# Two transformer blocks on one core: latent attention's values unit before the exponentials, a rotary unit in another bank, a gate exponential moved

## What is computed

```python
def _mla(x, w_in, g_q, g_kv, w_uq, w_uk, w_uv, w_o, pos):
    h = x @ w_in
    c_q = _rmsnorm(h[..., :384], g_q)
    c_kv = _rmsnorm(h[..., 384:640], g_kv)
    k_r = _rope(h[..., 640:], pos)
    q = jnp.einsum('bsr,rhd->bshd', c_q, w_uq)       # 8 heads, 128 + 64
    q_n, q_r = q[..., :128], _rope(q[..., 128:], pos)
    # keys c_kv @ w_uk, values c_kv @ w_uv, 128 per head;
    # causal softmax of (q_n.k_n + q_r.k_r) * 192**-0.5, times the values, @ w_o
```

## Time and profile before

| what | us |
|---|---|
| median of 3 runs | 2496.05 (2494.08 to 2497.16) |
| the profiled execution | 2496.92 |
| its span in the profile | 2495.1 |
| PE busy | 2433.2 (98%) |
| DVE busy | 1120.0 (45%) |
| ACT busy | 885.0 (35%) |
| mean granted clock of PE | 0.989 |

### The profile page before, as it was taken

One profiled execution on the slowest core, in us unless ns is written; L12 is line 12 of the kernel. 1 busy time (PEld: TensorE's weight loads), 2 busy tenths in 40 slices (PEclk: granted clock), 3 DMA queues, 4 the chain that ended last, 5 costly groups with the idle time before them and its releaser, 6 DMA issues.

```text
span 2495.1 us, 29378 instructions
## 1 busy us (share of the span) xinstructions
PE 2433.2 (98%) x11724; PEld 2015.2 (81%) x11724; DVE 1120.0 (45%) x1536; ACT 885.0 (35%) x1449; POOL 72.4 (3%) x146
## 2 busy tenths in 40 slices
PE   8889999999989999998999999999999999999998
PEld 7668888888878888887888888888877888888887
DVE  4556543346656443347454322233246624433334
ACT  4333332233534232235344323332245534522222
POOL 3000000000000000000000000000000000000000
PEclk9989999999989999999999999999999999999999
DMA  4121523323202322332222232222321122332332
GB/s 137 37 85 51 190 97 101 101 86 111 75 17 85 118 91 95 101 102 68 68 84 69 100 101 85 84 68 86 105 68 52 52 100 77 110 101 85 101 101 68
DMA packets 177048, 219.05 MB, mean 88 GB/s; under 512 B 9987, under 2 KB 131040, under 8 KB 176816
## 3 DMA queue, kind: packets, MB, share of 16 engines
q1 hardware_dynamic: 173152, 204.82, 25.4%
q0 software_dynamic: 3792, 12.75, 1.6%
HBM read 215.43 MB, written 5.27 MB: 88 GB/s over the span
## 4 chain that ended last, share of the span: by engine, by line
PE 92%; DVE 5%; ACT 2%; issue 1%; DMA 0%; SPq 0%; DVEq 0%; ACTq 0%
PE A L533 46%; PE B L533 42%; DVE WL L1871 1%; PE C L533 1%; ACT WH L1287 1%; PE C L955 0%; DVE ar L1939 0%; PE C L813 0%; DVE Y L2059 0%; PE C L1177 0%; DMA X<-in_x 0%; PE C L1015 0%; PE A L658 0%; DVE XL L1886 0%; DVE X L2477 0%
## 5 line engine op out<-in xcount | busy, mean ns | idle before, releaser
L1871 DVE TENSOR_TENSOR WL<-RAW,WH 128x2048 fp32r<-128x2048 f32 (+3 forms) x197 | 439.2, 2229 | 646.7 <-ACT WH L1287 646.5
L1287 ACT ACTIVATE WH<-RAW 128x2048 fp32r<-128x2048 f32 (+3 forms) x197 | 366.9, 1863 | 610.7 <-PE A L533 555.9
L533 PE MATMUL B<-XH,WH 128*128 128x512 f32 (+1 forms) x1432 | 544.4, 384 | 4.9 <-ACT ar L1290 2.6
L533 PE MATMUL B<-XH,WL 128*128 128x512 f32 (+1 forms) x1432 | 536.2, 378 | 0.0
L533 PE MATMUL B<-XL,WH 128*128 128x512 f32 (+1 forms) x1432 | 521.3, 379 | 2.8 <-DVE XL L1886 2.5
L533 PE MATMUL A<-WH,YH 128*128 128x512 f32 x944 | 368.0, 390 | 1.6 <-DVE YL L2404 1.6
L533 PE MATMUL A<-WH,YL 128*128 128x512 f32 x944 | 367.6, 389 | 0.0
L533 PE MATMUL A<-WL,YH 128*128 128x512 f32 x944 | 367.5, 389 | 0.0
L533 PEld LDWEIGHTS B<-XH,WH 128*128 128x128 f32 x1432 | 270.0, 189 | 72.5 <-issue 17.1
L533 PEld LDWEIGHTS B<-XH,WL 128*128 128x128 f32 x1432 | 270.1, 189 | 50.6
L533 PEld LDWEIGHTS B<-XL,WH 128*128 128x128 f32 x1432 | 260.7, 189 | 52.9 <-DVE XL L1886 4.8
(11 more groups left out here) (304 smaller groups left out, 2122.5 us busy)
## 6 DMA issues: line engine op xcount, KB each, us to landing
RAW<-in_w_in SPq DMA_DIRECT2D x33, 1024.0 KB, 5.2
RAW<-in_mlp_w_up SPq DMA_DIRECT2D x32, 1024.0 KB, 5.3
RAW<-in_mlp_w_down SPq DMA_DIRECT2D x32, 1024.0 KB, 5.0
RAW<-in_w_in SPq DMA_DIRECT2D x48, 512.0 KB, 4.4
RAW<-in_w_ffn_in SPq DMA_DIRECT2D x22, 1024.0 KB, 5.1
RAW<-in_w_ffn_out SPq DMA_DIRECT2D x10, 1024.0 KB, 5.0
RAW<-in_mla_w_o SPq DMA_DIRECT2D x4, 1024.0 KB, 5.1
RAW<-in_swa_w_q SPq DMA_DIRECT2D x4, 1024.0 KB, 5.1
```

The source lines that it names most:

```text
L533: return nc.tensor.matmul(dst, l, r, start=first, stop=last)
L1287: nc.scalar.activation(WH[s][:, 0:n], RAW[s][:, 0:n], ACT.Copy).then_inc(hi_ready, 1)
L1871: tt(WL[s][:, 0:n], RAW[s][:, 0:n], f32(WH[s][:, 0:n]), ALU.subtract).then_inc(lo_ready, 1)
```

## The change

1. `queries_by_feature` takes a list. Blocks 0 and 1 are transposed where all three were; block 2 comes inside `in_keys(1)`, behind its first token block.
2. Unit 4 of pair 0 has no number any more and lies in bank A3; its semaphore is `rope_taken`. The other units move up by one, so pair 0's units 2 and 5 lie in B0 and 3 and 6 in B1, and ten units alternate in place of eleven (`PAIR_AHEAD`).
3. Before the loop ACT splits the first chunk of pair 1 ahead of taking out unit 5, and DVE ahead of taking out unit 6; DVE normalises block 0 before the maxima of block 1.
4. In the loop ACT takes out a unit (0, 2 or 5) before the exponentials of step j+2, and in steps 1, 5 and 9 DVE makes the maxima before it splits.
5. At the start of the mLSTM ACT copies the two feature banks and splits a chunk before it makes the gates' exponential.

```diff
     def unit_number(i, u):
-        return PAIR_UNITS * i + tuple(units_in_order(i)).index(u)
+        return PAIR_UNITS * i - 1 + u if i else (0, 1, 2, 3, None, 4, 5)[u]
...
     def unit_bank(n):
-        return n % 2 if n < PAIR_AHEAD else 0
+        if n is None:
+            return A[3]
+        return B[n % 2 if n < PAIR_AHEAD else 0]
...
-    PAIRS, PAIR_STEPS, PAIR_UNITS, PAIR_AHEAD, PART_STEPS = 4, 16, 7, 11, (10, 11, 13, 14)
+    PAIRS, PAIR_STEPS, PAIR_UNITS, PAIR_AHEAD, PART_STEPS = 4, 16, 7, 10, (10, 11, 13, 14)
...
                 elif kh == 1:
                     r.then_inc(s_("in_kv"), 1)
+                    if t == 0:
+                        queries_by_feature((2,))
...
-        queries_by_feature()
+        queries_by_feature((0, 1))
         in_keys(1)
...
-            if n >= PAIR_AHEAD:
-                pe.wait_ge(*unit_taken(n - 1))
+            if n is None:
+                pass
+            elif n >= PAIR_AHEAD:
+                pe.wait_ge(*unit_taken(n - (2 if n == PAIR_AHEAD else 1)))
...
         # ACT
         pair_unit(0, 2)
+        split(c0 + 2, more=16 * 2 + 128)
         pair_unit(0, 5)
-        split(c0 + 2, more=16 * 2 + 128)
         pair_exp(0)
...
-            if j + 2 < PAIR_STEPS:
-                pair_exp(j + 2)
             for u in us[:1]:
                 if u in (0, 2, 5):
                     pair_unit(i, u)
+            if j + 2 < PAIR_STEPS:
+                pair_exp(j + 2)
             pair_hi(j)
...
+        before_conv(0, 0)
+        split_pair("ml", 0, 0, False)
         act.wait_ge(s_("if_m"), 1)
         nc.scalar.activation(G_EM, G_EM, ACT.Exp, scale=-1.0).then_inc(s_("if_g"), 1)
-        before_conv(0, 0)
-        split_pair("ml", 0, 0, False)
         after_conv(0, 0)
...
         # DVE
-        for u in (4, 3, 6):
-            pair_unit(0, u)
+        pair_unit(0, 4)
+        pair_unit(0, 3)
         split(c0 + 2)
+        pair_unit(0, 6)
         pair_max(0)
         pair_unit(1, 1)
         split(c0 + 3)
+        pair_normal(0)
         pair_max(1)
         pair_unit(1, 3)
-        pair_normal(0)
...
             pair_weights(j)
+            if j + 2 < PAIR_STEPS:
+                pair_max(j + 2)
             if j in (1, 5, 9):
                 split(c0 + 4 + j // 2)
-            if j + 2 < PAIR_STEPS:
-                pair_max(j + 2)
```

More of the change, by code:

```diff
@@ L239, in slot, with place_in_pair @@
         return c % 2
-    def units_in_order(i):
-        return (0, 1, 4, 2, 3, 5, 6) if i == 0 else range(PAIR_UNITS)
     def unit_number(i, u):
-        return PAIR_UNITS * i + tuple(units_in_order(i)).index(u)
+        return PAIR_UNITS * i - 1 + u if i else (0, 1, 2, 3, None, 4, 5)[u]
+    def place_in_pair(i, u):
+        return u if i else (0, 1, 3, 4, 2, 5, 6)[u]
     def wait_unit(e, i, u):
-        at = unit_number(i, u) - PAIR_UNITS * i
+        at = place_in_pair(i, u)
         if at in (4, 6):
@@ L257, in unit_bank @@
     def unit_bank(n):
-        return n % 2 if n < PAIR_AHEAD else 0
+        if n is None:
+            return A[3]
+        return B[n % 2 if n < PAIR_AHEAD else 0]
     def unit_taken(n):
+        if n is None:
+            return s_("rope_taken"), 2
         if n < PAIR_AHEAD:
             return s_("pair_u%d" % (n % 2)), n // 2 + 1
-        return s_("pair_u0"), (PAIR_AHEAD + 1) // 2 + n - PAIR_AHEAD + 1
+        return s_("pair_u0"), PAIR_AHEAD // 2 + n - PAIR_AHEAD + 1
     def units_of(j):
@@ L714, in in_keys, with queries_by_feature @@
                     r.then_inc(s_("in_kv"), 1)
-        def queries_by_feature():
-            for k in range(3):
+                    if t == 0:
+                        queries_by_feature((2,))
+        def queries_by_feature(ks):
+            for k in ks:
                 u = n0 + 2 + k
@@ L756, in pair_unit @@
             sl, n = slot(c), unit_number(i, u)
-            bank = B[unit_bank(n)]
+            bank = unit_bank(n)
             if u in (0, 5):
                 pe.wait_ge(lo_ready, c + 1)
-            if n >= PAIR_AHEAD:
-                pe.wait_ge(*unit_taken(n - 1))
+            if n is None:
+                pass
+            elif n >= PAIR_AHEAD:
+                pe.wait_ge(*unit_taken(n - (2 if n == PAIR_AHEAD else 1)))
             elif n >= 2:
@@ L770, in pair_unit @@
                     for k in range(2):
-                        if n == 5 and x == 0:
+                        if n == 4 and x == 0:
                             pe.wait_ge(c_free[(in_c + 5 + k) % 2], (in_c + 5 + k) // 2 + 1)
@@ L780, in pair_unit @@
                 for k in range(nk):
-                    if n < 5:
+                    if i == 0:
                         cu = in_c + 2 + x0 + k
@@ L784, in pair_unit @@
                     r = mm3(bank[:], wh[:, k, at:at + P], wl[:, k, at:at + P], YH[:, x0 + k, :], YL[:, x0 + k, :], k == 0, k == nk - 1)
-            r.then_inc(chunk_done if n - PAIR_UNITS * i in (4, 6) else s_("pair_f"), 1)
+            r.then_inc(chunk_done if place_in_pair(i, u) in (4, 6) else s_("pair_f"), 1)
         def pair_scores(j):
@@ L791, in pair_scores @@
             if q == 0:
-                for x in (3, 4):
-                    pe.wait_ge(*unit_taken(PAIR_UNITS * i + x))
+                for u in (2, 3):
+                    pe.wait_ge(*unit_taken(unit_number(i, u)))
                 pe.wait_ge(s_("qr_ready"), i + 1)
@@ L819, in pair_values @@
                 for u in (5, 6):
-                    pe.wait_ge(*unit_taken(PAIR_UNITS * i + u))
+                    pe.wait_ge(*unit_taken(unit_number(i, u)))
             if j == 0:
-                pe.wait_ge(*unit_taken(PAIR_AHEAD - 2))
+                pe.wait_ge(*unit_taken(PAIR_AHEAD - 1))
             pe.wait_ge(s_("pair_lo"), j)
@@ L836, in output_part @@
                 pe.wait_ge(lo_ready, c + 1)
-                pe.wait_ge(*unit_taken(PAIRS * PAIR_UNITS - 1))
+                pe.wait_ge(*unit_taken(unit_number(PAIRS - 1, PAIR_UNITS - 1)))
                 pe.wait_ge(s_("pair_lo"), 8)
```

## The result

| | before | changed |
|---|---|---|
| median | 2495.12 us of 4 runs (2494.08 to 2497.16) | 2464.61 us of 4 runs (2463.94 to 2468.89) |
| the profiled execution | 2496.92 | 2468.89 |
| span | 2495.1 | 2467.1 |
| granted clock, mean | 0.989 | 0.993 |

The ratio is 0.988, with a 95% interval of 0.9868 to 0.9891: faster by 1.2%. The forecast was 2468.0 with a range of 2464.5 to 2474.0. Profile against profile, as the sum was made, the gain is 2496.92 - 2468.89 = 28.0 us against a sum of 28.4.

What follows compares the result with a forecast made beforehand. TensorE (PE) was taken as the bound, so only its waits and slow clock give time back. Gains 1.1 + 4.6 + 1.3 + 17.3 + 4.1 = 28.4 us off 2496.9 gave 2468.5, written as 2468.0 for the median; range 2464.5 to 2474.

Steps and rivals of the forecast that it cites:

- (a): Query latents: third transposition behind the first token block of in_keys(1) removes PE's wait for bank C0; gain 1.1 us.
- (b): First pair: rotary unit in A3 and earlier splits remove waits and clock loss, leaving a new 0.8 us wait; gain 4.6.
- (c): First normalisation on DVE ahead of the second maxima and unit 3's copy in pair 1 removes PE's wait; gain 1.3 us.
- (d): Loop steps 1, 5, 9: ACT copies unit 5 before exponentials, so long waits and slow clock go; gain 17.3 us together.
- (e): Start of the mLSTM: bank copies ahead of the gates' exponential remove PE's 2.6 us wait and 1.5 of clock; gain 4.1.
- a long wait is thus paid twice: Behind PE's long waits the clock is 0.51 to 0.65, a second payment of 1.5 to 2.6 us each.
- the 0.9 us between execution and median: Whole kernel: the profiled execution lies 0.9 us above the runs' median, so 2468.5 would be a median of 2467.6.
- 1, the clock low behind short waits: First pair and loop: clock stays low behind waits of 0.2 to 0.8 us, 8.5 us not returned, 2477; chance 0.07.
- 2, DVE in ACT's place: Loop: unit 6's copy ends a filled DVE queue, 1 us more delay in three steps, 2471 to 2472; chance 0.09.
- 3, part (e) without gain: Start of the mLSTM: copies wait for something else or ACT is late for the first head, 2472; chance 0.04.
- 4, exponentials behind the units: Loop steps 1, 2, 3, 5, 6, 7: PE comes to wait for delayed exponentials, slower at 2502; chance 0.01.

Runs made afterwards that it cites:

- the gates' run: Kernel before with only the gates' exponential moved behind the two bank copies and the split: 2490.11 us, ratio 0.9983.
- ACT's half: Kernel before with only ACT's loop order changed, the unit taken out before the exponentials of step j+2: 2479.64 us, ratio 0.9936.
- DVE's half: Kernel before with only DVE's loop order changed, maxima ahead of the split: 2485.38 us, ratio 0.996.
- both halves: Kernel before with the loop's ACT and DVE orders both changed and nothing else: 2475.69 us, ratio 0.992.
- the kernel with four copies: Changed kernel with four copies of a small constant onto itself on ACT before taking out unit 5 in steps 1, 5, 9: 2464.22 us, ratio 0.9882.

## Why the prediction was right

Part by part, from PE's timelines. A row is a distance between two places in PE's program, and its difference is the gain there:

| part | from, to | before | after | gain | forecast |
|---|---|---|---|---|---|
| (a) | transposed latents (C, L723) to unit 0 | 8.41 | 7.05 | 1.4 | 1.1 |
| (b) | unit 0 to unit 0 of pair 1 | 19.44 | 14.81 | 4.6 | 4.6 |
| (c) | from there to its rotary unit | 13.21 | 11.46 | 1.8 | 1.3 |
| (d) | values(j) to the next unit 0, step 1 | 10.09 | 4.79 | 5.3 | 5.2 |
| | the same, step 5 | 10.88 | 4.78 | 6.1 | 6.1 |
| | the same, step 9 | 11.18 | 5.15 | 6.0 | 6.0 |
| (e) | from the splits, in the gates' run | 52.8 | 48.4 | 4.4 | 4.1 |

These make 29.6 us; less the 1.8 at 1100 us they are 27.8, where the profiles differ by 28.0.

**Right: the order of what is late next.** Part (b) forecast a new wait of 0.8 us behind unit 5, from DVE's chain of two instructions of 0.7; it is 0.79 (0.79 and 0.78 in the two runs that change the first pair alone). Part (d) forecast leftovers of 0.2, 0.2 and 0.6; they are 0.17, 0.18 and 0.54. What made this possible is that each queue is filled around these places, so the durations of the earlier trace rows could simply be added up.

**Slightly off: (a) and (c)**, 0.3 and 0.5 us too small: the term was mis-sized since I counted only the wait that the profile names, and a wait costs more. PE's timeline around it in the kernel before:

```profile
79.06 0.39 PE L533 MATMUL B<-YH,WL 128*128 128x512 f32 x1
80.72 0.69 PE L813 MATMUL C<-ident,ar 128*128 128x128 f32 x2 [1.27 <-DVE ar L1984]
81.25 0.81 PE L533 MATMUL A<-ar 128*128 128x384 f32 x2
```

and in the changed kernel:

```profile
73.65 0.40 PE L537 MATMUL B<-YH,WL 128*128 128x512 f32 x1
73.88 0.38 PE L821 MATMUL C<-ident,ar 128*128 128x128 f32 x2
```

with the scores right behind at 74.10. From the last product to the transposes it was 1.66 us and is 0.23: 1.27 of wait and 0.16 by which matmuls that follow each other overlap. From the transposes to the scores it was 0.53 and is 0.22: the first instructions behind a wait run 0.31 longer. Together 1.27 + 0.16 + 0.31 = 1.74, the gain measured. In (a) it is 1.13 + 0.16 and 0.06 at the transposes (0.41 from 44.76 to the next block, now 0.35 from 45.50).

**Off in kind, though not in sum: "a long wait is thus paid twice".** I took the clock's part as a fixed price of each long wait, 10.0 us of the 28.4. For this pair of profiles that holds to a few tenths. But the runs show it is no fixed price: the first pair's wait of 2.2 us costs 1.7 us of clock in the kernel before, and nothing in those with ACT's half, DVE's half, both halves or the gates alone, where nothing ahead of it was changed. In the one with ACT's half 1.7 us were lost behind the split's wait of 1.6 us instead, which I had counted as free. So 1.7 us of part (b)'s 4.6 depend on the execution that they are compared with. A sum over parts tried alone is wrong by 2.7 us in 28 for that reason.

**The median.** 30.5 us of gain against 28.0 between the profiles: the other three executions of the changed kernel lie 4.0 to 5.0 us below the profiled one, at mean clocks of 0.995 to 0.996 against its 0.993. The second profile of the changed kernel shows where such an execution gains it, outside the places that the change touches. So the forecast of 2468.0 was right for the profiled execution and 3.4 too high for the median. The median of 2464.61 lies only 0.1 us above the lower end of the range, with 5 us between the executions, so that it lies inside is partly luck. The step at fault is the one that carried the 0.9 us between execution and median of the kernel before over to the new one.

**The rivals.** 1, the clock low behind short waits: in the latent attention of the changed kernel it is 1.00 at all of them, and still behind the added waits of 0.74 us. But the ground on which I gave the rival 0.07, no loss behind waits of 1.3 and 1.5 us, was too thin. The trace of the kernel before has such waits in the sliding-window attention too (1.54, 1.27 and 1.28 us, ending at 716.22, 720.76 and 727.39), and there the clock is low:

```profile
720.00:730.00 10.00, 7.96 (x37) 7.62 (x37) 1.98 (x6) 1.92 (x8) 0.00 (x0) 0.50 0.01 2
```

In the kernel with four copies the wait of 2.67 us that ends at 682.38 there cost nothing (1.00 from 682.4 to 687 us), and the clock fell only after waits of 1.06, 1.40 and 1.27 us that followed each other every 4 us:

```profile
690.00:710.00 20.00, 16.18 (x111) 15.08 (x112) 11.53 (x24) 9.04 (x26) 0.00 (x0) 0.91 0.00 1
```

The Trainium skill ("TensorE: Matmul & The Clock Gate", section "A second HAM failure mode: psum-queue depth-cycling") tells that brief idling between groups of matmuls keeps throwing the clock back. The trace of the sliding-window attention agrees with that (0.50 from 720 to 730 us); in the latent attention it did not show behind single waits of 0.7 and 0.8 us.

2, DVE in ACT's place: this happens where DVE's half is left out (1.5, 1.5 and 1.9 us), so the rival's mechanism is real, and the swap of maxima and split is what removes it. 3, part (e) without gain: refuted by the gates' run, where the wait is gone and 4.4 us with it. 4, exponentials behind the units: no wait of PE on an exponential appears.

**What stays open.** Why the same waits in the sliding-window attention cost 10.5 us of clock in one execution, 7.0 in another and 1.4 in the kernel with four copies. The change moves the time at which that stage begins, but the two executions of the changed kernel differ as well, so it is not the program alone. No run here separates the two. Open for the same reason is why a single wait of 1.6 to 2.2 us is followed by a fall in one kernel and not in another; whether the waits ahead of it count, as those of the sliding-window attention suggest, was not tried.

## What to carry to other kernels

In an in-order queue, put the instruction that frees the bottleneck engine's next buffer ahead of the one that itself still waits, and then look at the other queue: here ACT's half of the loop left 1.5 to 1.9 us per pair on DVE, DVE's half 1.9 on ACT, and both together 0.2 to 0.5. Add up the durations of the queue's rows up to the copy that frees the bank, and take the time at which the bottleneck engine comes for it from its own rows; that gave the changed kernel's leftover waits to 0.1 us. Count a wait's clock loss as a range from nothing up to the loss that the profile shows, not as a fixed price, and do not count a single wait of 1.6 us, or several of 1.1 to 1.4 us in a row, as free; judge parts of under 0.2% by a local stretch of the timeline, since the clock elsewhere moves the whole time by more.

## What the hardware showed that I had not expected

- Waits of the same length can cost different amounts. PE's single waits in the attention of all the profiles (40 to 180 us), by length, and how many of them saw the granted clock fall during the wait or within 2 us behind it: 0.7 to 1.0 us, 0 of 14; 1.1 and 1.3 us, 0 of 14; 1.5 and 1.6 us, 1 of 9; 1.8 us, 2 of 3; 1.9 us, 1 of 4; 2.2 us, 2 of 6 (both executions of the kernel before); 2.8 us, 3 of 3; 3.7 to 4.1 us, 15 of 15. One fall cost PE between 1.4 and 2.9 us.
- In the sliding-window attention, where waits of 1.1 to 1.5 us follow each other some 4 us apart, the clock was low behind them, once for a whole 10 us (0.50 from 720 to 730 us in the kernel before).
- Two executions of the kernel before gave the same clock in the four places of the latent attention to 0.01, and two of the changed kernel differed by 5.7 us, 5.3 of them through the clock elsewhere.
- A wait of PE costs up to 0.5 us more than its row says: 0.16 of overlap with the instruction ahead, and 0.06 to 0.31 in the first short matmuls behind it.
- A copy of 128x128 on ACT onto itself, each waiting for the one ahead, takes 0.33 us (four in 1.33).
